# Row weights join the row-number table, and the four first gathers go ahead of the second expert's weights

## What is computed

```python
def hier_moe(h, p):
    gl = h @ router_group_w + router_group_b                 # 4 groups
    gsel = argmax(gl); gw = softmax(gl)[gsel]
    el_sel = (h @ router_expert_w + router_expert_b)[..., gsel, :]   # its 4 experts
    top_v, top_i = top_k(el_sel, 2)
    tw = softmax(top_v) * gw
    ...
    for e in range(16):
        he = silu(h @ expert_w_gate[e]) * (h @ expert_w_up[e])        # 1024 -> 512
        y = y + gate[..., e:e+1] * (he @ expert_w_down[e])            # 512 -> 1024
```

## Time and profile before

| | us |
|---|---|
| median of 3 runs | 1444.5 |
| the profiled execution, its own time | 1442.75 |
| its span | 1441.0 |
| PE busy | 1340.0 (93%) |
| DVE / ACT / POOL busy | 470.5 / 347.4 / 496.8 |
| mean granted TensorE clock | 0.947 of full speed |

### The profile page before, as it was taken

How to read it: one execution, slowest core, us unless ns; L and a number is a source line. 1 busy time by engine, 2 the same in 40 slices (tenths; PEclk the granted TensorE clock), 3 DMA queues, 4 the chain that set the end, 5 groups by cost and what they waited for, 6 DMA issues and landing times. The chain is left out here.

```text
span 1441.0 us, 34971 instructions
## 1 busy us (share of the span) xinstructions
PE 1340.0 (93%) x14649; PEld 951.3 (66%) x14649; DVE 470.5 (33%) x1180; ACT 347.4 (24%) x798; POOL 496.8 (34%) x753
## 2 busy tenths in 40 slices
PE   6999999799999999999999699997799999999990
PEld 5666666466665688888888455545577777777770
DVE  3025634222222255545555210215222222222223
ACT  4003111222334323333332122221111111111114
POOL 8000000000000355555554202010466666666662
PEclk9999999899999979999999899997899999999996
DMA  6111111111110100000000741136989989799837
GB/s 183 30 30 45 31 30 44 29 30 30 30 30 20 29 3 9 10 10 10 9 10 15 232 167 60 58 93 211 367 257 320 343 273 373 250 313 372 248 84 262
DMA packets 116437, 178.25 MB, mean 124 GB/s; under 512 B 15360, under 2 KB 63991, under 8 KB 116330
## 3 DMA queue, kind: packets, MB, share of 16 engines
q1 hardware_dynamic: 100200, 155.89, 31.3%
q0 software_dynamic: 15936, 20.57, 7.0%
q10 hardware_dynamic: 194, 0.23, 0.1%
HBM read 149.47 MB, written 27.19 MB: 123 GB/s over the span
## 5 line engine op out<-in xcount | busy, mean ns | idle before, releaser
L360 PE MATMUL ps<-hT,w_in 128*128 128x352 f32 (+1 forms) x1296 | 396.5, 465 | 0.8 <-DVE conv_state_T L708 0.8
L360 PEld LDWEIGHTS ps<-hT,w_in 128*128 128x128 f32 x1296 | 247.1, 191 | 140.5 <-issue 4.5
L2520 POOL DMA_INDIRECT sum_rows<-slot_out,scatter_rows x76 | 121.9, 1604 | 38.8 <-POOL scatter_rows L2519 26.0
L2565 PE MATMUL ps<-qkv,slot_T 128*32 128x256 f32 x1920 | 112.8, 386 | 3.7 <-DVE slot_T L2653 2.9
L2653 DVE TENSOR_TENSOR slot_T<-slot_raw_T,vecs 128x256 f32<-128x256 f32 x75 | 32.8, 438 | 215.7 <-PE ps L2565 215.6
L332 POOL DMA_DIRECT2D out_gdn_conv_prompt<-vbn x1 | 0.5, 521 | 297.1 <-ACT vbn L643 297.1
L2565 PEld LDWEIGHTS ps<-qkv,slot_T 128*32 128x32 f32 x1920 | 76.3, 112 | 34.1 <-issue 5.8
L2498 POOL DMA_INDIRECT gathered<-h_rows,gather_rows x79 | 83.9, 1062 | 19.9 <-issue 13.1
L2565 PE MATMUL ps<-cb,slot_T 128*32 128x256 f32 x1408 | 80.6, 379 | 0.0
L2609 ACT ACTIVATE slot_silu<-ps 128x128 f32<-128x128 f32 x77 | 21.5, 279 | 229.9 <-PE ps L2565 227.6
L2565 PEld LDWEIGHTS ps<-cb,slot_T 128*32 128x32 f32 x1408 | 55.5, 110 | 20.5
(11 more groups left out here) (634 smaller groups left out, 2235.2 us busy)
## 6 DMA issues: line engine op xcount, KB each, us to landing
w_in<-in_w_in SPq DMA_DIRECT2D x28, 512.0 KB, 4.0
qkv<-in_expert_w_gate SPq DMA_DIRECT2D x6, 2048.0 KB
qkv<-in_expert_w_up SPq DMA_DIRECT2D x6, 2048.0 KB
qkv<-in_expert_w_down SPq DMA_DIRECT2D x6, 2048.0 KB
cb<-in_expert_w_gate SPq DMA_DIRECT2D x5, 2048.0 KB
cb<-in_expert_w_up SPq DMA_DIRECT2D x5, 2048.0 KB
zg<-in_expert_w_down SPq DMA_DIRECT2D x5, 2048.0 KB
third_w_down<-in_expert_w_down SPq DMA_DIRECT2D x5, 2048.0 KB
```

The costliest lines, as they stand in the source:

```text
L360: last = pe.matmul(pbank(b)[:, c, 0:n], w[:, k, :], hT[:, k, c * CH:c * CH + n], start=(k == 0), stop=(k == KD - 1))
L2520: pool.indirect_dma_start(quarter_sums, bass.IndirectOffsetOnAxis(ap=sidx[:, r:r + 1], axis=0), y[r][:], None, compute_op=ALU.add).then_in ...
L2565: last = pe.matmul(gu_bank[c4[c], 0:2 * QF].rearrange("p (x b d) -> p x b d", x=2, d=32), xT[:, k, :], of_quarter(by_block[u][k], c), star ...
```

## The change

It moves the five small weight instructions of DVE into `output_stage`, behind `first`. `Aid` becomes 64 columns wide: POOL writes row numbers into columns 0 to 31, DVE writes row weights into columns 32 to 63, and one set of 18 products with `Bcol` fills both tables on 64 partitions. `i4` gets a second identity on partitions 32 to 63; a second spreading product and a copy make `route.weight` before the block ends. `experts` loses its products, copies and the waits on them. POOL issues four gathers first, and SP waits for the first to land before `load(1)`. `Aid` moves into the free end of `g.ub`; the comparison's scratch gets a buffer of its own.

```diff
-                      i4=F.sb("ident_by_head", NS, H, NS),
+                      i4=F.sb("ident_by_head", 2 * NS, H, NS),
...
+        pairs_of = T.sb("pairs_of_choices", P, 2 * TILES, ROWS_SLOT)
+        Aid = g.ub[:].rearrange("p a n -> p (a n)")[:, 2 * TILES * ROWS_SLOT:6 * TILES * ROWS_SLOT].rearrange("p (a n) -> p a n", n=2 * ROWS_SLOT)
...
+        table_w = ps[:, 7, 128:128 + TABLE]
+        once = place[0:2 * ROWS_SLOT].rearrange("p c t n -> p (c t n)")[:, 0:TABLE]
...
-                pool.tensor_copy(i4[:], bc(m.ident[0:NS, 0:NS], 1, H))
+                pool.tensor_copy(i4[0:NS], bc(m.ident[0:NS, 0:NS], 1, H))
                 pool.tensor_copy(l4[:], bc(m.lev[0:NS, 1, 0:NS], 1, H)).then_inc(s.i4, 1)
+                pool.tensor_copy(i4[NS:2 * NS], bc(m.ident[NS:2 * NS, NS:2 * NS], 1, H))
+                pool.drain()
...
-                    pool.tensor_tensor(Aid[:, of_c], Arow[:, of_c], behind[:], ALU.mult).then_inc(s.id, 1)
+                    pool.tensor_tensor(Aid[:, of_c, 0:ROWS_SLOT], Arow[:, of_c], behind[:], ALU.mult).then_inc(s.id, 1)
...
                     pe.wait_ge(s.id, c + 1)
+                    pe.wait_ge(s.rw, c + 1)
                     pe.wait_ge(s.slot, c + 1)
                     for a in range(c * TILES, c * TILES + TILES):
-                        last = pe.matmul(table[0:ROWS_SLOT], Aid[:, a, :], Bcol[:, a, :], start=(a == 0), stop=(a == 2 * TILES - 1))
+                        last = pe.matmul(table[0:2 * ROWS_SLOT], Aid[:, a, :], Bcol[:, a, :], start=(a == 0), stop=(a == 2 * TILES - 1))
...
+                pe.matmul(table4, by_group(i4[0:NS]), once[0:NS], start=True, stop=True).then_inc(s.table, 1)
+                pe.matmul(table_w, by_group(i4[NS:2 * NS]), once[NS:2 * NS], start=True, stop=True).then_inc(s.table, 1)
...
+                dve.wait_ge(s.ex, 2)
+                step(dve.tensor_reduce, den[:], route.exps[:, :, 0:NG], AX_X, ALU.add)
+                step(dve.scalar_tensor_tensor, den[:], route.exps[:, :, NG], 1.0, den[:], ALU.add, ALU.mult)
+                step(dve.reciprocal, route.w[:, 0], den[:])
+                step(dve.tensor_tensor, route.w[:, 1], route.exps[:, :, NG], route.w[:, 0], ALU.mult)
+                step(dve.tensor_scalar, route.w[:, :, NT], route.w[:, :, NT], route.valid[:], None, ALU.mult)
                 dve.wait_ge(s.rank, 1)
...
+                dve.wait_ge(s.row, 1)
                 for c in range(2):
                     of_c = slice(c * TILES, c * TILES + TILES)
+                    dve.tensor_tensor(Aid[:, of_c, ROWS_SLOT:2 * ROWS_SLOT], Arow[:, of_c], bc(route.w[:, c], 2, ROWS_SLOT), ALU.mult).then_inc(s.rw, 1)
                     dve.tensor_tensor(Bcol[:, of_c], bc(iota[:, 0:TABLE], 1, TILES), bc(sk[:, c], 2, TABLE), ALU.is_equal).then_inc(s.slot, 1)
...
                 dve.tensor_scalar(route.token[:], table4, quad[:], None, ALU.add)
+                dve.wait_ge(s.table, 3)
+                dve.tensor_copy(route.weight[:], table_w)
...
+                sp.wait_ge(in_ring[0], 16)
                 load(1)
                 sp.wait_ge(s.xg, 1)
-                sp.wait_ge(s.wt, 1)
...
-                    gather((r + RING - 1) % RING)
+                    if copies is not None or r:
+                        gather((r + RING - 1) % RING)
                     pool.tensor_copy(xg[:], ring[r][:]).then_inc(s.xg, 1)
...
-                for r in range(RING - 1):
+                for r in range(RING):
                     gather(r)
```

More of the change, by code:

```diff
@@ L1587 @@
 o y on ysc yn oT bon yT sout tokm vm sc dS Sup dz zadd zdec zo zof st_out w x0 x1 wr wrn out x2 h2 h2p hT hTd h2o0 h2o1 lg lgd rs chosen tot rank
-exd ex row slot id table once""".split()
+exd ex row rw slot id table once""".split()
 def sample_views(g):
@@ L1646, in output_stage @@
         spare = T.sb("spare_rows", P, ROWS_SLOT)
-        Aid = T.sb("row_choice_ids", P, 2 * TILES, ROWS_SLOT)
+        pairs_of = T.sb("pairs_of_choices", P, 2 * TILES, ROWS_SLOT)
+        Aid = g.ub[:].rearrange("p a n -> p (a n)")[:, 2 * TILES * ROWS_SLOT:6 * TILES * ROWS_SLOT].rearrange("p (a n) -> p a n", n=2 * ROWS_SLOT)
+        den = T.sb("r_choice_den", P, TILES)
         Arow, Bcol = row_choice_views(g)
@@ L2163, in _ @@
                 dve.memset(xy[NS:2 * NS, NT, :], 0.0).then_inc(s.zeros, 1)
-                dve.memset(Aid[:], 0.0)
+                dve.memset(pairs_of[:], 0.0)
                 dve.memset(before_t[:, 0], 0.0)
@@ L2286, in choose @@
                     n = (t1 - t0) * (1 + NG)
-                    pair = Aid[:].rearrange("p a n -> p (a n)")[:, 0:16 * n].rearrange("p (s k) -> p s k", k=16)
+                    pair = pairs_of[:].rearrange("p a n -> p (a n)")[:, 0:16 * n].rearrange("p (s k) -> p s k", k=16)
                     for d in range(1, EPG):
@@ L2366, in _ @@
                 dve.wait_ge(s.table, 1)
-                dve.tensor_copy(once, table[0:ROWS_SLOT]).then_inc(s.once, 1)
+                dve.tensor_copy(once, table[0:2 * ROWS_SLOT]).then_inc(s.once, 1)
                 dve.wait_ge(s.table, 2)
@@ L2422, in experts @@
         idx, sidx = route.idx, T.sb("scatter_rows", P, RING, dt=U32)
-        sum_of, other, den = T.sb("slot_sums", P, TABLE, dt=U32), T.sb("spare_rows_by_slot", P, TABLE), T.sb("choice_den", P, TILES)
-        once = T.sb("row_weights_by_slot", ROWS_SLOT, TABLE)[:]
+        sum_of, other = T.sb("slot_sums", P, TABLE, dt=U32), T.sb("spare_rows_by_slot", P, TABLE)
         xg = T.sb("slot_quarters", P, QD)
@@ L2547, in _ @@
             def _(pe):
-                pe.wait_ge(s.wq, 1)
-                for a in range(2 * TILES):
-                    last = pe.matmul(ps[0:ROWS_SLOT, 7, 0:TABLE], row_weights[:, a, :], slot_onehot[:, a, :], start=(a == 0), stop=(a == 2 * TILES - 1))
-                last.then_inc(s.wt, 1)
-                pe.wait_ge(s.wc, 1)
-                pe.matmul(ps[:, 7, 128:128 + TABLE], route.i4[:].rearrange("p h n -> p (h n)"), once, start=True, stop=True).then_inc(s.wt, 1)
                 pe.sem_inc(s.xTp, 1)
@@ L2665, in _ @@
                     dve.memset(other[:].rearrange("p (i r) -> p i r", r=RING)[:, :, a], 4.0 * ROWS_SLOT * a)
-                dve.tensor_reduce(den[:], route.exps[:, :, 0:NG], AX_X, ALU.add)
                 dve.drain()
-                dve.scalar_tensor_tensor(den[:], route.exps[:, :, NG], 1.0, den[:], ALU.add, ALU.mult)
                 dve.scalar_tensor_tensor(other[:], route.token[:], 4.0 * NTOK - 0.5, other[:], ALU.is_ge, ALU.mult)
                 dve.drain()
-                dve.reciprocal(route.w[:, 0], den[:])
                 dve.tensor_tensor(sum_of[:], route.token[:], other[:], ALU.add)
                 dve.drain()
-                dve.tensor_tensor(route.w[:, 1], route.exps[:, :, NG], route.w[:, 0], ALU.mult)
                 dve.tensor_copy(sidx[:, 0:1], sum_of[:, 0:1]).then_inc(s.st, 1)
-                dve.drain()
-                dve.tensor_scalar(route.w[:, :, NT], route.w[:, :, NT], route.valid[:], None, ALU.mult)
-                dve.drain()
-                dve.tensor_tensor(row_weights, row_weights, bc(route.w[:].rearrange("p c t -> p (c t)"), 2, ROWS_SLOT), ALU.mult).then_inc(s.wq, 1)
-                dve.wait_ge(s.wt, 1)
-                dve.tensor_copy(once, ps[0:ROWS_SLOT, 7, 0:TABLE]).then_inc(s.wc, 1)
-                dve.wait_ge(s.wt, 2)
-                dve.tensor_copy(route.weight[:], ps[:, 7, 128:128 + TABLE]).then_inc(s.wtd, 1)
                 rows_T(0, first=True)
```

10 lines of the change are left out of this document (3 added, 7 removed).

## The result

| | before | after |
|---|---|---|
| median, us (4 executions each) | 1443.5 | 1433.47 |
| ratio, with its 95% interval | | 0.994 (0.992 to 0.9959) |
| the profiled execution, its own time | 1442.75 | 1432.39 |
| its span | 1441.0 | 1430.7 |
| `rank` starts | 997.34 | 991.90 |

The forecast was 1442.4, with a range down to 1439.9. The kernel gained 10 us, and the range doesn't hold it. The table divides the 10.3 us by which the two spans differ: 5.44 us arise ahead of `rank`, where the change does nearly nothing, 5.31 us between `rank` and the second `gate_up`, and 0.45 us are lost behind it, after the last `gate_up`.

What follows compares the result with a forecast made beforehand. The start and speed of the first `gate_up` were taken as the bound, with POOL waiting for PE's signal. -3.16 + 0.8 + 0.25 = -2.1 us, from 1444.5 to 1442.4 us; range 1439.9 to 1446.0.

Steps and rivals of the forecast that it cites:

- POOL's start: Start of `experts`: first gather to the quarters' copy falls from 9.23 to 6.07 us without PE's products, gain 3.16.
- The loop bound: POOL's load of its loop bound before the first row numbers, no longer hidden by idle time: 0.7 us, between 0 and 3.4.
- Table operands: Before the table products: DVE's two extra products of 288 elements make PE start 0.45 or 1.15 us late, taken as 0.8.
- The rule of turns: Table operands: DVE and POOL take turns for whole instructions, costing 0.45 us with DVE first, 1.15 with POOL first.
- 64 columns: The 18 table products on PE: 64 columns instead of 32 cost 0 us, since weight loads overlap the products.
- The rival that rested on them: Slower: loading 64 columns costs what 128 do, so the table products take 3.3 us more; 1446.0 us, chance 0.07.
- Five small steps: DVE's five small weight instructions, 1.3 us, hide in its 2.22 us of idle time before `rank`: no cost.
- Weight copy: The copy behind DVE's two index writes, ahead of the barrier, makes everything start later by about 0.25 us.
- SP's wait: SP issues `load(1)` behind the first gather, about 1015 us; with some 20 us of slack this changes nothing.
- the rival on the landing: The quarters wait up to 7.6 us for the first gather to land, gain only 1.3: 1444.2 us, chance 0.09.
- Clock: PE's clock rises 4.7 us behind a start: table products 0.5 us longer, first `gate_up` 0.6 less, together 0.
- more than that: Rival: DVE first, loop bound nearly free at 0.2, clock earlier in `gate_up`; gain 3.3 us, 1441.2, chance 0.33.

Runs made afterwards that it cites:

- the kernel with early quarters: The changed kernel with the first slot's row numbers and quarters copied ahead of the third gather, SP waiting for the second gather: 1435.28 us, ratio 0.9956.

## Why the prediction was wrong

What bounds the stage was read right: the start of the first `gate_up` and its speed, and a microsecond there arrives whole: the last `gate_up` stands 5.30 us nearer to `rank` too. The sum of -2.1 has -5.3 in its place. By its terms:

- *POOL's start*, -3.16, measured -4.21. The loop bound, priced at 0.7, costs nothing that the trace shows; the rest is the row numbers, which overlap the quarters by 0.07 where a gap of 0.1 had been counted, and gathers of 0.95 to 0.97 instead of 1.02.
- *Table operands*, +0.8 as the mean of 0.45 and 1.15, measured +0.52: DVE went first. The rule of turns (the Trainium skill, SBUF — State Buffer, "Who interferes with whom") gave 0.45 for this order, and the trace agrees with it within 0.1.
- *64 columns*, 0, as measured: the table's products are 0.2 shorter, but by the clock. The rival that rested on them is refuted.
- *Five small steps*, 0, as measured. *Weight copy*, +0.25: it takes 0.26, and from the end of the table's products to the first gather the distance grows by 0.17 (2.32 to 2.49).
- *SP's wait*, "Nothing". This is the step that failed as reasoning: the wait is worth 2.9 us. I asked of it only whether `load(1)` would be late, and it isn't. I didn't ask what the weights did to the gather: 7.0 to 7.2 us to land beside them, at most 2.8 to 3.1 ahead of them. The sum used the right landing (under 5.08), so its number does not suffer; but it credits to PE's removed products what needed both edits. The change without the wait gives 2.5, the wait alone 0.05, both together 5.3. I had the right thought in the rival on the landing, as an argument against it, and did not carry it back to the term.
- *Clock*, "Together 0" (+0.5 in the table's products, -0.6 in the first `gate_up`), measured -0.2 and -1.5. I took the spread of the clock's return for luck and used a mean of 4.7 us behind the start; it came 3.1 and 2.9 behind. In four profiles of the changed kernel the first `gate_up` takes 4.99 to 5.04 us, in three with the old start 6.54 to 6.57: it repeats with the kernel. This is the step that failed by size, the largest of all: 1.7 us of the 3.2 that the sum lacks.

Of the difference between 2.1 and 5.3 us, 1.7 are the clock, 1.05 POOL's start, 0.3 the operands, 0.1 the copy. The rival *more than that* (3.3 us, chance 0.33) was the nearest, and its 1441.2 still lies 2 us above what the section gives (1444.5 - 5.3 = 1439.2, itself 0.7 under the range). The rest of the 10 us of the first measurement comes from ahead of `rank`, where its cause stays open. The range had nothing in it for such a part, although the three times of before already spread over 2 us and the prediction counted from one profiled execution 1.75 under their median.

What would show it right came out for the chain (no PE products before `gate_up`, quarters behind the first gather with POOL busy, no wait at expert 1), and wrong for "about 2 us" (the first `gate_up` came 3.8 us nearer to `rank`); the table's products, 4.89 us, fell just under their 5 to 6.4. Two readings of rows were slightly off and change nothing: the first rise of the earlier trace rows is 3.6 us behind its start and not 3.7, and 36 loads of 0.23 make 8.3 and not 8.4.

## What to carry to other kernels

Where an engine waits for two things, the profile names the one that ended last; before costing an edit, work out when the other ended, or the gain stops there. A small gather issued beside a large stream of weights landed some 4 us late here (7.0 to 7.2 us from its start instead of 3.1 or less), so hold a stream that is not urgent until the urgent small transfer is in. When a start on PE moves, price its first group of matmuls at the clock that it will find; where PE idles ahead of a critical group, matmuls that nobody reads, few enough to end before the operands come, can be worth more than shortening the chain (1.3 us against 0.6 at the second `gate_up` here).

## What was not expected of the hardware

- The landing of a 128-row gather issued by POOL depends on SP's transfers: 6.97 and 7.22 us from its start with 6 MB of weights issued 0.75 us ahead of it, 2.93, 2.98 and 2.77 us or less (the second gather of the kernel with early quarters) with the weights held back. The Trainium skill (DMA: Bandwidth & Descriptors, "Queues, rings and completion order") says that each DMA engine goes round between the queue rows that have work and drains a whole packet before it switches. That fits a small transfer which is slowed but not stopped; no view here shows in which order packets went.
- The clock granted to PE was 1.00 when PE went idle behind the table and 0.50 before 8 us had passed; with PE kept busy there it stayed at 1.00 up to `gate_up` in all six runs. Elsewhere it was less simple: ahead of the rank sums, where the four (or nine) matmuls began at 1.00, it fell to 0.50 all the same and then rose (rank sums at 0.95 and 1.00, 0.50 without them), and behind the short set it fell once more between ranks and table (0.50 in the stretches of 999 to 1001). What decides there is open. The Trainium skill (TensorE: Matmul & The Clock Gate, "HAM oscillation — how this bites in real kernels") says that waits between groups of matmuls bring the clock down; the runs agree, and add that work without use holds it up.
